# Hybrid encoder block on one core: p's projection moved two experts later, overflow buffer moved

## The chip, the cores and the metric

The kernel runs on one core of one Trainium2 chip. The metric is the device time of one launch in microseconds; the time before is the median of three runs. Everything is float32.

## The reference, cut to what matters

One layer, 512 tokens of 1024 values. After a pooling and state-space mixer, 32 experts follow (4 groups of 8), of which each token takes two; then a gated projection of a side input p, and a last norm:

```python
    h = h + concat([a, s]) @ W_out
    h = h + HierarchicalMoE(RMSNorm(h))      # top-1 group, then top-2 experts in it
    gate = jax.nn.sigmoid(rmsnorm(h, g_ple[i]) @ ple_gate_w[i] + ple_gate_b[i])
    h = h + gate * (p[i] @ ple_proj_w[i])    # p: 512 x 256, ple_proj_w: 256 x 1024
return rmsnorm(h, g_final)
```

An expert is `silu(v @ w_gate) * (v @ w_up) @ w_down` with w_gate and w_up of 1024 x 256 and w_down of 256 x 1024. The change concerns `p[i] @ ple_proj_w[i]`, which depends on nothing else in the layer.

## The kernel before, in words

The five engines each have a program written out by hand; the order of the work on an engine is the order of its code, and semaphores join the engines. The stage that matters is the loop over the 32 experts (`for e in range(1, NE)` at L1980 on TensorE).

Each expert gets a slot of 64 token rows (`CAP`). Its weights come as three pieces of 1 MB (gate, up, down), 96 in all; SyncE issues them in order (`weights`, `load_piece`, L356), each as soon as the buffer that it goes to has been used up (`SPOT`, `AFTER`). The tokens' rows are gathered for two experts at a time by GpSimd (`gather`, L1499) and each expert's result of 128 x 512 values is scattered to DRAM by GpSimd (`scatter`, `rows_out`, L1504) from one of three buffers (`M_Y`, `e % YBUF`). This is done for experts 0 to 29; experts 30 and 31 are combined on TensorE from their buffers (`combined`).

TensorE's steps, all through the helper of L1578 unless another line is given: `gu_step(e)` is the gate and up product (16 matmuls of 64 x 256), `h_step(e)` a transpose (L1940), `down_step(e)` the down product (4 matmuls of 64 x 512), `x_step` 8 transposes of token rows for the next two experts (L1921). One turn of the loop is `h_step(e)`, `x_step` on even e, `gu_step(e + 1)`, now and then a piece of p's work, `down_step(e)`. The trace records every float32 matmul of the products twice (a `gu_step` is x32, a `down_step` x8), a transpose once.

p's work in the loop: at e = 19 (`P_ROWS`) p is transposed (`p_rows`, L1888). At e = 21, 23, 25 and 27 (`P_PROJ`) two half tiles of the projection are computed (`proj`, 2 x 2 matmuls of 128 x 512, banks 0 and 6 of `PP_BANK`, x8 in the trace). ScalarE copies each half tile to zbuf (`pp_out`, L529), between `silu` of the next expert (L752) and the copy of this expert's result (`y_out`, L529). The next `x_step` uses the same banks and waits for these copies (`pp_done`, L1986). The result is read only in the last stage (L1572, L1358).

Behind the experts: GpSimd waits until all scatters have landed and sets `moe_done` by a memset (L1567). SyncE waits for `moe_done` and for `down_step(30)` and then issues the read back of the scattered pairs (`load_pairs(0)`, L492), half of the gate's weights, and the rest. VectorE adds the pairs to h (`combine`, L1330, then L854 with the product of experts 30 and 31), TensorE turns h (`turned_h`, L2036), VectorE scales it to ut (L854), and `gate(0)` to `gate(7)` follow on TensorE.

If an expert has more than 64 tokens, a second loop of rounds follows on every engine (behind `most(...) > CAP`). It gathers, computes and scatters through one slot.

Of the kernel before, what the change touches and what calls it, by code (L numbers as in the profile page):

```python
# [50 lines left out]
NE = NG * NEG  # L51
# [5 lines left out]
PIECE = 2048  # L57
NPIECE = 22
LOADS = 8
YBUF = 3  # L60
# [38 lines left out]
def at(t, parts, off, dims):  # L99

    p0, p1 = parts
    width = t.shape[1]
    return bass.AP(t, p0 * width + off, [[width, p1 - p0]] + [list(d) for d in dims])


def dr(a, off, dims):

    return bass.AP(a.tensor, off, [list(d) for d in dims])
# [25 lines left out]
def build(nc, A, out):  # L134
    ctx = ExitStack()
    with ctx:
        def sb(name, width, dt=F32):
            return ctx.enter_context(nc.sbuf_tensor(name, [P, width], dt))

        def sem(name):  # L140
            return ctx.enter_context(nc.semaphore(name))
# [4 lines left out]
        ALL = (0, P)  # L146
# [6 lines left out]
        moe = sb("moe", 6144)  # L153
# [11 lines left out]
        sidx_o = sb("sidx_o", 1, I32)  # L165
# [5 lines left out]
        bank = [ctx.enter_context(nc.psum_tensor(f"bank{k}", [P, 512], F32)) for k in range(8)]  # L171
# [33 lines left out]
        M_XT, M_SG, M_HT, M_Y, M_XG = 0, 2048, 2304, 2560, 4096  # L205
# [5 lines left out]
        for name, n in (("pr", NT * 32), ("pa", 2 * NT * 32), ("px", NT * 32), ("gm", NT), ("d4", NT * 4), ("e4", NT * 4), ("gs", NT), ("gp", NT),  # L211
# [60 lines left out]
        xT_ps, xT_sb, gu_ps, sg_sb, hg_sb, hT_ps, hT_sb, dn_ps, dn_sb = (  # L272
            sem(n) for n in ("xT_ps", "xT_sb", "gu_ps", "sg_sb", "hg_sb", "hT_ps", "hT_sb", "dn_ps", "dn_sb"))

        o_w, o_tbl, o_idx, o_xg, o_st, o_turn = (sem("o_" + n) for n in ("w", "tbl", "idx", "xg", "st", "turn"))
# [21 lines left out]
                    at(bank[Y_BANK[b]], ALL, 0, [[P, 4], [CH, L], [1, CH]]))  # L297

        PP_BANK = (0, 6)
        P_ROWS, P_PROJ = 19, (21, 23, 25, 27)  # L300
        H_BANK = (0, 2, 4, 2)

        ROOT3 = tuple(NT + t + 1 for t in range(NT))
# [17 lines left out]
        E_PPW, E_PIN, E_PPT = 10 * PIECE, 11 * PIECE, 11 * PIECE + NT * DPLE  # L321
        NA = NT - 1
        E_WPLE = (8 * PIECE, 0)
        O_SLOT = 3 * PIECE
        E_S = E_PIN
        M_GF, M_BP = 4096, 5120

# [21 lines left out]
        def most(eng):  # L349

            return eng.value_load(at(flag, (0, 1), 0, [[1, 1]]), min_val=0, max_val=T)

        def load_piece(eng, e, k, to, done):

            w = (wg_d, wu_d, wd_d)[k]
            eng.dma_start(at(to[0], ALL, to[1], [[1, PIECE]]),  # L356
                          w[e].rearrange("(p j) f -> p (j f)", p=P)).then_inc(done, 16)
# [7 lines left out]
        def _(sp):  # L365
# [106 lines left out]
            with sp.If(most(sp) > CAP):  # L472
                with sp.Fori(1, ROUNDS) as r:
                    with sp.Fori(0, NE) as e0:
# [3 lines left out]
                        for k in range(3):  # L478
                            load_piece(sp, e, k, (ring, O_SLOT + k * PIECE), o_w)
                sp.wait_ge(o_w, 48 * NE * (ROUNDS - 1))  # L480
# [45 lines left out]
        def _(act):  # L526

            def copy(o, i, signal):
                act.activation(o, i, ACT.Copy).then_inc(signal, 1)  # L529
# [260 lines left out]
            with act.If(most(act) > CAP):  # L790
                act.wait_ge(dn_sb, NE)
                with act.Fori(1, ROUNDS) as r:
                    with act.Fori(0, NE) as e:
                        turn = act.snap((r - 1) * NE + e + 1)
                        count = act.snap(turn + NE)
                        act.wait_ge(gu_ps, count)
                        act.activation(at(moe, (0, CAP), M_SG, [[1, DE]]), at(bank[1], (0, CAP), 0, [[1, DE]]),
                                       ACT.Silu).then_inc(sg_sb, 1)
                        act.wait_ge(dn_ps, count)
                        copy(at(moe, ALL, M_Y, [[1, 512]]), bank[4][:, :], dn_sb)  # L800
            with act.Else():
                pass

# [596 lines left out]
        def _(pool):  # L1400
# [97 lines left out]
            def rows_in(k, index, done):  # L1498
                pool.indirect_dma_start(at(moe, ALL, M_XG + k * DM, [[1, DM]]), None, v_d,  # L1499
                                        bass.IndirectOffsetOnAxis(ap=index, axis=0),  # L1500
                                        bounds_check=T - 1, oob_is_err=False).then_inc(done, 16)

            def rows_out(k, index, done):
                pool.indirect_dma_start(pairs, bass.IndirectOffsetOnAxis(ap=index, axis=0),  # L1504
                                        at(moe, ALL, M_Y + k * 512, [[1, 512]]), None,
                                        bounds_check=4 * T - 1, oob_is_err=False).then_inc(done, 16)
# [27 lines left out]
            def note(k):  # L1534

                return pool.tensor_tensor(at(fill, (0, 1), 4 + k, [[1, 1]]), at(fill, (0, 1), 0, [[1, 1]]),
                                          at(fill, (0, 1), 1, [[1, 1]]), ALU.add)

            with pool.If(most(pool) > CAP):
                pool.wait_ge(slot_done, 1)  # L1540
                for c in range(2 * NT):
                    pool.indirect_dma_start(tbl_d, bass.IndirectOffsetOnAxis(ap=slot_i[:, c:c + 1], axis=0),
                                            pair_i[:, c:c + 1], None).then_inc(tbl_set, 16)
                pool.wait_ge(tbl_set, 16 * 2 * NT)
                note(3).then_inc(o_turn, 1)
                with pool.Fori(1, ROUNDS) as r:
                    with pool.Fori(0, NE) as e:
                        turn = pool.snap((r - 1) * NE + e + 1)
                        dma16 = pool.snap(turn * 16)
                        both = pool.snap(turn * 2)  # L1550
                        count = pool.snap(turn + NE)
                        place = pool.snap(r * (CAP * NE))
                        pool.wait_ge(o_turn, turn)
                        for k in range(2):
                            pool.dma_start(at(tblw, (k * CAP, (k + 1) * CAP), 0, [[1, NE]]),
                                           dr(tbl_d, place, [[NE, CAP], [1, NE]])).then_inc(o_tbl, 16)
                        pool.wait_ge(o_idx, both)
                        note(0)
                        rows_in(0, gidx_o[:, 0:1], o_xg)
                        pool.wait_ge(dn_sb, count)  # L1560
                        note(1)
                        rows_out(0, sidx_o[:, 0:1], o_st)
                        pool.wait_ge(o_st, dma16)
                        note(2).then_inc(o_turn, 1)
            with pool.Else():
# [10 lines left out]
        def _(pe):  # L1576
# [349 lines left out]
            def gate_up(k, odd, gate_w, up_w, dst, rows=0, between=None):  # L1926

                for j in range(KC):
                    if rows and j % 4 == 0:
                        pe.wait_ge(xT_sb, rows - 1 + j // 4)  # L1930
                    if between and j == 4:
                        between()
                    for n, w in enumerate((gate_w, up_w)):
                        last = mm(bank[dst][n * CAP:(n + 1) * CAP, 0:DE],
                                  at(moe, ALL, M_XT + k * DM + j * P + odd * CAP, [[1, CAP]]),
                                  at(w[0], ALL, w[1] + j * DE, [[1, DE]]), j == 0, j == KC - 1)
                return last
# [4 lines left out]
            def down(k, w, dst):  # L1942

                for j in range(2):
                    for n in range(2):
                        last = mm(bank[dst][n * CAP:(n + 1) * CAP, :], at(moe, ALL, M_HT + k * P + j * CAP, [[1, CAP]]),
                                  at(w[0], ALL, w[1] + j * DM + n * 512, [[1, 512]]), j == 0, j == 1)
                return last
# [48 lines left out]
            with pe.If(most(pe) > CAP):  # L1997
                with pe.Fori(1, ROUNDS) as r:
                    with pe.Fori(0, NE) as e:
# [9 lines left out]
                        pe.wait_ge(o_w, dma48)  # L2009
                        gate_up(0, 0, (ring, O_SLOT), (ring, O_SLOT + PIECE), 1).then_inc(gu_ps, 1)  # L2010
                        pe.wait_ge(hg_sb, h_count)
                        h_rows().then_inc(hT_ps, 1)
                        pe.wait_ge(hT_sb, count)
                        down(0, (ring, O_SLOT + 2 * PIECE), 4).then_inc(dn_ps, 1)
                pe.wait_ge(dn_sb, NE * ROUNDS)
# [57 lines left out]
```

## Time and profile before

| | us |
|---|---|
| median of 3 runs | 526.2 |
| lowest and highest | 523.4, 529.41 |
| the profiled execution's own time | 522.91 |
| its span, first to last instruction | 521.0 |
| TensorE busy in the span | 480.7 (92%) |
| VectorE, ScalarE, GpSimd busy | 240.9, 163.3, 159.8 |
| moved by DMA | 146.83 MB, mean 282 GB/s |
| mean granted TensorE clock | 0.984 |

The profile is of one execution. Its time is 1.9 us more than its span, and 3.3 us below the median of the three runs, which lie 6 us apart. A duration that is read from it belongs to the 522.91 us; a difference that is worked out from it is laid on the median.

### The profile page before, as it was taken

The page shows a single profiled execution, that of the slowest core. Times are in us where ns is not written, and L with a number is a line of the kernel's source. Part 1 is how long each engine was busy: PE and PEld are TensorE (multiplying, and loading weights), DVE is VectorE, ACT ScalarE, POOL GpSimd, SP SyncE. Part 2 cuts the span into 40 slices and gives each one's busy share as a digit, 9 for nine tenths or more (in the row PEclk, how much of TensorE's full clock was granted, in tenths as well). Part 3 has the DMA queues.
Part 4 walks back from the last instruction along what each step waited for, and adds up shares of the span by engine and source line. Part 5 has one row for each costly group of instructions (what it writes and reads, how often), then busy time and mean ns, then how long its engine had stood idle before and what let it go on. Part 6 is the DMA issues. An engine that isn't in the chain of part 4 may idle for free.

```text
span 521.0 us, 7294 instructions
## 1 busy us (share of the span) xinstructions
PE 480.7 (92%) x2743; PEld 270.9 (52%) x2743; DVE 240.9 (46%) x683; ACT 163.3 (31%) x264; POOL 159.8 (31%) x144
## 2 busy tenths in 40 slices
PE   0999999999999998979999999787999998899993
PEld 0655776734854477745555555444545543444441
DVE  2899998999233358642222222111111211474525
ACT  5643334456442344111111111121121121313464
POOL 1069999954100111222222222202102210003250
PEclk9999999999999999999999999998899998999998
DMA  8784300499289966999999999999999997970012
GB/s 297 141 195 87 75 0 1 147 141 209 110 340 423 414 274 226 403 410 405 422 416 419 419 414 412 422 417 419 423 418 418 419 418 300 350 307 0 0 81 81
DMA packets 57195, 146.83 MB, mean 282 GB/s; under 512 B 27722, under 2 KB 32870, under 8 KB 44360
## 3 DMA queue, kind: packets, MB, share of 16 engines
q1 hardware_dynamic: 50856, 133.92, 69.2%
q0 software_dynamic: 5904, 12.41, 6.2%
q8 instruction: 22, 0.36, 0.3%
q14 instruction: 13, 0.11, 0.1%
q10 hardware_dynamic: 400, 0.04, 0.1%
HBM read 138.17 MB, written 16.29 MB: 296 GB/s over the span
## 4 chain that ended last, share of the span: by engine, by line
PE 75%; DMA 17%; DVE 3%; ACT 2%; SPq 1%; issue 1%; ACTq 0%; DVEq 0%
PE bank L1578 68%; DMA big<-in_exp_w_up_dram 10%; DMA ring<-in_exp_w_up_dram 6%; PE bank L1921 2%; PE bank L1663 1%; DMA ring<-in_ssm_a_im_dram 1%; SPq L356 1%; PE bank L1940 1%; PE bank L1601 1%; ACT moe L529 1%; DVE moe L854 1%; PE bank L1807 1%; PE bank L2036 1%; DVE moe L1091 1%; ACT L537 0%
## 5 line engine op out<-in xcount | busy, mean ns | idle before, releaser
L1578 PE MATMUL bank<-ring,moe 128*64 128x256 f32 (+3 forms) x976 | 130.1, 392 | 3.3 <-DMA ring<-in_exp_w_up_dram 3.3
L1578 PEld LDWEIGHTS bank<-ring,moe 128*64 128x64 f32 (+1 forms) x976 | 76.9, 147 | 39.9 <-issue 17.2
L1504 POOL DMA_INDIRECT pairs_d<-moe,sidx_all x32 | 31.9, 998 | 160.5 <-PE bank L1921 81.6
L854 DVE TENSOR_TENSOR vrow<-moe,bank 64x128 f32<-64x128 f32 x64 | 18.6, 291 | 123.2 <-ACT moe L752 122.2
L1578 PE MATMUL bank<-big,ut 128*128 128x512 f32 x128 | 56.6, 595 | 1.0 <-ACT ut L674 1.0
L1578 PE MATMUL bank<-ut,big 128*128 128x512 f32 x128 | 57.4, 596 | 0.2 <-ACT ut L541 0.2
L752 ACT ACTIVATE moe<-bank 64x256 f32<-64x256 f32 x32 | 12.1, 378 | 143.2 <-PE bank L1578 143.2
L1578 PE MATMUL bank<-ring,ut 128*128 128x512 f32 x128 | 55.7, 593 | 0.4 <-DVE ut L854 0.4
L529 ACT ACTIVATE moe<-bank 128x512 f32<-128x512 f32 x56 | 32.6, 598 | 62.1 <-PE bank L1578 49.4
L1578 PE MATMUL bank<-big,moe 128*64 128x256 f32 (+1 forms) x264 | 44.9, 448 | 6.3 <-DMA zbuf<-in_exp_w_up_dram 3.1
L854 DVE TENSOR_TENSOR ring<-ring,bank 128x64 f32<-128x64 f32 (+1 forms) x142 | 39.5, 278 | 2.8
L1578 PEld LDWEIGHTS bank<-big,ut 128*128 128x128 f32 x128 | 23.9, 190 | 30.9 <-issue 30.6
L1578 PEld LDWEIGHTS bank<-ring,ut 128*128 128x128 f32 x128 | 24.0, 190 | 29.3 <-issue 29.3
L1578 PEld LDWEIGHTS bank<-ut,big 128*128 128x128 f32 x128 | 23.4, 190 | 25.5 <-issue 24.7
L854 DVE TENSOR_TENSOR bank<-bank,ring 128x64 f32<-128x64 f32 (+1 forms) x142 | 35.1, 287 | 2.9
L1578 PEld LDWEIGHTS bank<-big,moe 128*64 128x64 f32 x264 | 22.5, 145 | 22.0 <-issue 7.7
L1578 PE MATMUL bank<-ring 128*64 128x128 f32 (+1 forms) x128 | 32.5, 437 | 0.0
L1267 DVE COPY moe<-bank 128x128 f32<-128x128 f32 x32 | 9.3, 292 | 45.5 <-PE bank L1940 45.5
L854 DVE TENSOR_TENSOR moe<-bank,vec 128x512 f32<-128x512 f32 x40 | 25.9, 686 | 7.2 <-PE bank L1921 5.2
L1578 PEld LDWEIGHTS bank<-ring 128*64 128x64 f32 (+1 forms) x128 | 15.2, 163 | 15.3 <-issue 15.0
L1572 POOL TENSOR_TENSOR ring<-ring,zbuf 128x512 f32<-128x512 f32 x6 | 8.1, 1349 | 48.1 <-ACT ring L815 48.1
L529 ACT ACTIVATE zbuf<-bank 128x512 f32<-128x512 f32 x16 | 11.5, 718 | 34.5 <-PE bank L1578 34.5
(190 smaller groups left out, 605.5 us busy)
## 6 DMA issues: line engine op xcount, KB each, us to landing
ring<-in_exp_w_up_dram SPq DMA_DIRECT2D x19, 1024.0 KB, 30.2
ring<-in_exp_w_down_dram SPq DMA_DIRECT2D x18, 1024.0 KB, 29.9
ring<-in_exp_w_gate_dram SPq DMA_DIRECT2D x17, 1024.0 KB, 26.2
big<-in_exp_w_gate_dram SPq DMA_DIRECT2D x7, 1024.0 KB, 13.4
big<-in_exp_w_down_dram SPq DMA_DIRECT2D x7, 1024.0 KB, 12.8
big<-in_exp_w_up_dram SPq DMA_DIRECT2D x6, 1024.0 KB, 16.0
big<-in_w_in_dram SPq DMA_DIRECT2D x2, 2048.0 KB, 11.8
ut<-in_exp_w_gate_dram SPq DMA_DIRECT2D x4, 1024.0 KB
```

What stands on the lines that cost most here:

```text
L356: eng.dma_start(at(to[0], ALL, to[1], [[1, PIECE]]), w[e].rearrange("(p j) f -> p (j f)", p=P)).then_inc(done, 16)
L529: act.activation(o, i, ACT.Copy).then_inc(signal, 1)
L752: act.activation(at(moe, (0, CAP), M_SG, [[1, DE]]), at(bank[1 + e % 2], (0, CAP), 0, [[1, DE]]), ACT.Silu).then_inc(sg_sb, 1)
L854: return dve.tensor_tensor(o, a, b, op)
L1091: return dve.scalar_tensor_tensor(o, a, b, c, op0, op1)
L1267: dve.tensor_copy(at(moe, ALL, M_HT + (e % 2) * P, [[1, P]]), bank[3][:, 0:P]).then_inc(hT_sb, 1)
L1504: pool.indirect_dma_start(pairs, bass.IndirectOffsetOnAxis(ap=index, axis=0), at(moe, ALL, M_Y + k * 512, [[1, 512]]), None, bounds_check= ...
L1572: seq(pool.tensor_tensor(sg, sg, at(zbuf, ALL, n * 512, [[1, 512]]), ALU.mult))
L1578: return pe.matmul(o, a, b, start=start, stop=stop, skip_group_check=loose)
L1601: last = pe.transpose(bank[j][:, t * P:(t + 1) * P], at(moe, ALL, M_XN + t * DM + j * P, [[1, P]]), ident)
L1663: last = pe.transpose(bank[B_WT + ri][:, (g % 4) * P:(g % 4 + 1) * P], rv(R_W + ri * 1024 + g * P, P), ident)
L1921: last = pe.transpose(bank[j // 4 * 6][:, (j % 4) * P:(j % 4 + 1) * P], at(moe, ALL, M_XG + k * DM + j * P, [[1, P]]), ident)
```

## The change

Two things. The four pairs of half tiles of p's projection are computed at e = 23, 25, 27 and 29 in place of 21, 23, 25 and 27, on TensorE and, with their copies, on ScalarE. In the loop for overfull experts, the result goes through buffer 2 of `M_Y` (29 % 3) in place of buffer 0, on ScalarE and GpSimd.

```diff
         PP_BANK = (0, 6)
-        P_ROWS, P_PROJ = 19, (21, 23, 25, 27)
+        P_ROWS, P_PROJ = 19, (23, 25, 27, 29)
...
-        O_SLOT = 3 * PIECE
+        O_SLOT, O_Y = 3 * PIECE, (NE - 3) % YBUF
...
-                        copy(at(moe, ALL, M_Y, [[1, 512]]), bank[4][:, :], dn_sb)
+                        copy(at(moe, ALL, M_Y + O_Y * 512, [[1, 512]]), bank[4][:, :], dn_sb)
...
-                        rows_out(0, sidx_o[:, 0:1], o_st)
+                        rows_out(O_Y, sidx_o[:, 0:1], o_st)
```

On TensorE, in the turn of e = 21: 64x256 x16 is `gu_step(22)`, 128x512 x4 the two half tiles, 64x512 x4 `down_step(21)`, L1940 `h_step`.

```order
 L1940 MATMUL bank<-cst,vrow 128x128
 L1578 MATMUL bank<-ring,moe 64x256 x16
-L1578 MATMUL bank<-ring 128x512 x4
 L1578 MATMUL bank<-ring,moe 64x512 x4
 L1940 MATMUL bank<-cst,vrow 128x128
```

The half tiles are gone from here. The rows of e = 23, 25 and 27 read the same in both kernels, though they hold other half tiles.

On TensorE, in the turn of e = 29, of the kernel after the change: `h_step(29)`, `gu_step(30)`, half tiles, `down_step(29)`, `h_step(30)`, then `gu_step(31)` and `down_step(30)`.

```order
 L1940 MATMUL bank<-cst,vrow 128x128
 L1578 MATMUL bank<-ring,moe 64x256 x16
+L1578 MATMUL bank<-ring 128x512 x4
 L1578 MATMUL bank<-ring,moe 64x512 x4
 L1940 MATMUL bank<-cst,vrow 128x128
```

The last two half tiles now stand between `gu_step(30)` and `down_step(29)`, and so ahead of `gu_step(31)`.

On ScalarE, the end of the loop in the kernel after the change: `silu(30)`, the two `pp_out`, `y_out(29)`, `silu(31)`, `y_out(30)` and `y_out(31)`.

```order
L752 ACTIVATE moe<-bank 64x256
L529 ACTIVATE zbuf<-bank 128x512 x2
L529 ACTIVATE moe<-bank 128x512
L752 ACTIVATE moe<-bank 64x256
L529 ACTIVATE moe<-bank 128x512 x2
```

In the kernel before, nothing stands there between `silu(30)` and `y_out(29)`. The programs of VectorE, GpSimd and SyncE keep their order.

## Rows read from the trace of the kernel before

**Rows 1.** Page, 40 slices of the span: granted clock and DMA share in tenths.
```profile
PEclk9999999999999999999999999998899998999998
DMA  8784300499289966999999999999999997970012
```
**Rows 2.** Waits of TensorE, 300 to 521 us: us in total, times, longest.
```profile
PE bank L1578 <- DMA ring<-in_exp_w_up_dram: 3.3, 2, 3.1
PE bank L1578 <- DMA big<-in_exp_w_up_dram: 2.9, 2, 2.6
```
**Rows 3.** Timeline of TensorE: start, duration, line, tiles, records [idle before].
```profile
361.74 6.46 PE L1578 MATMUL bank<-ring,moe 128*64 128x256 f32 x32 [3.06 <-DMA ring<-in_exp_w_up_dram]
368.13 3.70 PE L1578 MATMUL bank<-ring 128*128 128x512 f32 x8
...
411.97 3.67 PE L1578 MATMUL bank<-ring,moe 128*64 128x256 f32 x32
415.58 3.70 PE L1578 MATMUL bank<-ring 128*128 128x512 f32 x8
419.21 1.94 PE L1578 MATMUL bank<-ring,moe 128*64 128x512 f32 x8
421.08 0.33 PE L1940 MATMUL bank<-cst,vrow 128*128 128x128 f32 x1
...
428.05 5.39 PE L1578 MATMUL bank<-ring,moe 128*64 128x256 f32 x40 [0.19 <-DMA ring<-in_exp_w_up_dram]
...
436.30 6.75 PE L1578 MATMUL bank<-big,moe 128*64 128x256 f32 x40 [2.59 <-DMA big<-in_exp_w_up_dram]
```
**Rows 4.** Stretches, TensorE: length, busy, granted clock, DMA share, GB/s.
```profile
343.30:346.00 2.70, 0.73 (x8) 1.00 1.01 416
346.00:352.00 6.00, 6.00 (x46) 1.00 1.01 417
...
434.00:436.30 2.30, 0.00 (x1) 0.87 1.01 404
436.30:439.00 2.70, 2.70 (x14) 0.50 0.77 305
439.00:441.80 2.80, 2.80 (x26) 0.98 0.45 176
```
**Rows 5.** The chain that ended last, up to the gate: start, us, what.
```profile
405.17 31.09 DMA big<-in_exp_w_up_dram
...
446.42 7.21 PE bank L1578 x32
453.63 0.60 PE bank L2036 x4
```
**Rows 6.** Timeline of VectorE behind the experts.
```profile
449.18 2.99 DVE L1330 SCALAR_TENSOR_TENSOR h<-big,small,h 128x512 f32<-128x512 f32 x4 [5.54 <-DMA big<-pairs_d]
452.28 1.29 DVE L854 TENSOR_TENSOR h<-bank,h 128x512 f32<-128x512 f32 x2
454.25 1.29 DVE L854 TENSOR_TENSOR ut<-bank,vec 128x512 f32<-128x512 f32 x2 [0.69 <-PE bank L2036]
...
462.67 1.29 DVE L854 TENSOR_TENSOR ut<-bank,vec 128x512 f32<-128x512 f32 x2 [2.64 <-PE bank L2036]
```
**Rows 7.** Instructions on the scattered pairs: ns min/median/max, first and last start.
```profile
L1504 POOL DMA_INDIRECT pairs_d<-moe,sidx_all x32: 982/992/1043, 226.7 to 434.9; - x32
```
**Rows 8.** Timelines of ScalarE and GpSimd at the last scatter.
```profile
433.49 0.60 ACT L529 ACTIVATE moe<-bank 128x512 f32<-128x512 f32 x1 [1.34 <-PE bank L1578]
...
434.86 0.98 POOL L1504 DMA_INDIRECT pairs_d<-moe,sidx_all  x1 [4.86 <-ACT moe L529]
441.79 0.09 POOL L1567 MEMSET fill<- 1x1 int32 x1 [5.95 <-issue]
```
**Rows 9.** Timeline of SyncE: the issue of the first pairs.
```profile
443.14 0.34 SPq L492 DMA_DIRECT2D big<-pairs_d  x1
```
**Rows 10.** DMA issues, 300 to 521 us: count, KB each, us to landing.
```profile
out_dram<-ring SPq DMA_DIRECT2D x2, 256.0 KB, 2.0
```

## The prediction

> **What bounds the kernel now.** I read the page first. Its slices show DMA busy at 9 tenths from about the middle to slice 33 and TensorE's clock full but for a few slices [rows 1]: the expert stage sits close to both limits. Next come TensorE's waits in the second part of the span: it waits only for expert weights, a few us in all [rows 2]. Then the timeline places them [rows 3]: 3.06 us ahead of gu_step(22) at 361.74, 0.19 ahead of gu_step(30) at 428.05, and 2.59 ahead of gu_step(31) at 436.30. Between 361.74 and 428 TensorE never waits, so there it is the bound by a hair; at either end the weights are. From gu_step(22) to gu_step(31) are 9 experts in 436.30 - 361.74 = 74.56 us, 8.28 us each. As both of these starts are landings of weights, 8.28 us is the pace at which an expert's 3 MB arrive; it puts gu_step(30)'s at 361.74 + 8 x 8.28 = 428.0, where the row has 428.05. The DMA share of 1.01 in a sample stretch [rows 4] agrees. The piece that gu_step(31) waits for was issued at 405.17 and took 31.09 us to land [rows 5]: a long queue, so what TensorE does a few us earlier or later does not change when weights land.
>
> The chain that ended last then goes straight through TensorE: the combination of experts 30 and 31 from 446.42, turning h from 453.63, then VectorE's scaling at 454.25 and the gate's products [rows 5, 6]. About that place VectorE matters too: the pairs land and it starts at 449.18, and it is done with h at 452.28 + 1.29 = 453.57 [rows 6], within 0.1 us of when TensorE is free at 453.63. Two chains arrive there together, and the change lengthens one of them.
>
> **The change, part by part.** Overflow buffer: costs nothing. There are 32 scatters in the trace [rows 7], which are the 30 of experts 0 to 29 and the two of zeros ahead of them, so the loop for overfull experts does not run; one constant changes in it.
>
> Half tiles out of e = 21: 415.58 to 419.21 is 3.63 us for two half tiles in front of down_step [rows 3]. The same work at 368.13 to 371.8 goes. TensorE then has 3.63 us in hand from there on. It can't keep them: at the arrival pace of 8.28 us per expert, gu_step(24)'s weights land at 378.3, those for 26 at 394.9, for 28 at 411.4. gu_step(28) starts at 411.97 [rows 3], only 0.5 us behind that. So the lead is given back as small waits in front of gu_step(24), (26), (28) and (30). For gu_step(30) I work this out: from gu_step(28) to being ready for gu_step(30) takes 428.05 - 0.19 - 411.97 = 15.89 us; from 411.45 that is 427.3, a wait of 0.7 us for 428.05. If nothing had been given back the wait would be 0.19 + 3.63 = 3.8 us. I take 0.7, since the pace holds within 0.1 us at gu_step(30). The SyncE issues behind these steps gain nothing, by the queue of 31 us.
>
> Half tiles into e = 29: gu_step(30) starts at 428.05 as before, since it waits for weights. It takes 3.61 us (411.97 to 415.58), then half tiles 3.63, down_step(29) 1.87 (419.21 to 421.08), and some 0.26 for h_step(30) (0.33 by its row at 421.08, of which the next step covers a little). That is 428.05 + 9.37 = 437.42 for gu_step(31). Its weights have been there since 436.30. Cover of 2.59 us plus what is left of it: the half tiles are hidden but for 1.12 us.
>
> The clock: before, gu_step(31) and down_step(30) took 6.75 us for the 40 records that take 5.39 warm [rows 3], because the granted clock is 0.50 in that stretch, which is 1.2 GHz, right behind the idle 2.59 us [rows 4]. After, TensorE works from 428.05 to 443 without a gap over 0.1 us, so I price this at 5.33 us plus nothing: 1.36 us won back. down_step(30) ends at 437.42 + 5.33 = 442.75, where before it was 436.30 + 6.75 = 443.05. The new wait of 0.7 us ahead of gu_step(30) I price at nothing: an idle 1.98 us up to 345.27 left the clock at 1.00, in the stretch of the gap and in the one behind it [rows 4]. On TensorE alone the change comes to -0.3 us.
>
> The last scatter: this is what pays. ScalarE's copy of expert 29's result starts when down_step(29) ends, at 433.49 before, and the scatter at 434.86 [rows 8], 1.37 us later. Now down_step(29) ends at 437.16, the copy starts at 437.27 (both pp_out are over by 436.1, 0.6 us each, behind half tiles that end by 435.3), and the scatter at 438.64, 3.78 us later. Before, GpSimd's memset followed the scatter's start by 6.93 us (0.98 of work and 5.95 idle until it landed) [rows 8], and at 441.79 it was 1.2 us earlier than needed, since SyncE also waits for down_step(30) and issued the pairs at 443.14 [rows 9]. Now: with the same 6.93 us the memset is at 445.57 and the pairs are issued at 445.7, 2.6 us late. From the other side, a store of 256 KB, as large as the scatter, landed in 2.0 us when DMA had nothing else to move [rows 10]; then the memset is at 441.6, down_step(30) decides again, and the issue is 0.3 us early. The DMA load behind 438.6 lies between: share 0.77 up to 439.0, 0.45 up to 441.8, against 1.01 around the old scatter's start [rows 4]. The nearest row is the old scatter itself, with the same rows, queue and target, so I stay by its side and take 5.0 us to landing: memset at 444.6, pairs issued at 444.8, 1.65 us late. The rule of the Trainium skill (DMA: Bandwidth & Descriptors, "Anatomy of one DMA") gives a DMA some 2.0 us and its bytes at 436 GB/s, 2.6 us here, by which the scatter would land ahead of down_step(30) and the whole change would be worth -0.3 us; the 5.95 us of the trace speak against it, with load on the engines.
>
> What follows: the pairs land 1.65 us later, VectorE starts at 450.8 and has h done at 455.2 in place of 453.57. It scaled h at 454.25 before, held by TensorE's transposes for 0.68 us [rows 5, 6]; this slack is used up first. gate(0) therefore starts 1.65 - 0.68 = 1.0 us later. Behind it TensorE is the bound, as the loads issued behind the pairs move by the same 1.65 us, and VectorE stood idle for 2.64 us ahead of the next tile's scaling [rows 6].
>
> The sum: TensorE -0.3, hidden behind the pairs' +1.0; so 522.91 + 1.0 = 523.9 for an execution like the profiled one, and 526.2 + 1.0 = 527.2 on the median. The median lies 3.3 us above the profiled execution, and its runs 6 us apart. What a measurement of this kernel can tell from no change is about 1%, 5.3 us, five times my figure. Bounds of the terms: pairs from -0.3 to +2.6 - 0.7 = +1.9 us.
>
> **The rivals.**
> *The half tiles are fully covered (A).* If the scatter lands in 3 us or less, or if the last weights are late by some us more (the median execution is 3.3 us longer than the profiled one, and DMA is the natural cause), down_step(30) decides the issue of the pairs and TensorE's own balance counts: -0.3 us to -1.4 us with the clock kept, 525.5 us. For it: DMA load falls off just there. Against it: 5.95 us of landing.
> *The clock and the pairs (B, slower).* The place is gate(0). If TensorE's wait ahead of gu_step(30) is long enough to bring the clock down there (it is up to 3.8 us if weights come unevenly; 3.06 us ahead of gu_step(22) did, with 6.46 us for what takes 3.67 [rows 3]), gu_step(31) is 1.36 us later still. The scatter too, so that with its old 6.93 us the pairs are issued 2.6 + 1.4 = 4.0 us late and gate(0) starts 3.3 us late. TensorE has by then been idle for over 2.6 us, and pays 1.4 to 2.8 us of low clock in gate(0), the prices of the falls at 436.30 and 361.74. Sum +4.7 to +6.1, 531.6 us. It decides where the wait ahead of gu_step(30) has grown from my 0.7 us to one like that of 2.59 us, which the low clock followed, and is no longer like that of 1.98 us. The Trainium skill (TensorE: Matmul & The Clock Gate, Part 1) says that where the clock turns varies from run to run of the same kernel; by that some executions pay and some don't. No run yet shows this.
> *The weights come earlier (C).* If TensorE's lead of 3.63 us freed buffers that SyncE waits for, the last weights could land up to 3.6 us earlier: -2.5 us, 523.7 us. Against it: 31 us from issue to landing of the last one [rows 5]; a queue that long is not short of issues.
>
> **How the numbers follow.** Forecast 0.50 (527.2, own range 525.9 to 528.1), A 0.28, B 0.12, C 0.05, something unforeseen 0.05. The range must hold the medians' own scatter, whose three runs span 523.4 to 529.41, laid about A to B: 523.2 to 531.0. Slower by over 1% (above 531.5): half of B and a little noise, 0.08. Faster by over 1% (below 520.9): hardly reached even by C, 0.04 with noise. The rest, 0.88, is within 1%.
>
> **What would show it.** Right, step by step, if in the profile of the changed kernel the wait of about 3 us ahead of gu_step(22) stands, gu_step(24), (26), (28) and (30) have waits of 0.5 to 1.6 us, gu_step(31) has none and takes 3.6 us at clock 1.00; if the last scatter starts 3.8 us later, the memset follows it by about 6 us, and the pairs are issued by it and not by down_step(30); and if VectorE's wait for the pairs ends 1 to 2 us later. Wrong if gu_step(31) still waits (then weights come later than I hold), if the memset is ahead of down_step(30)'s end (A), if the clock is 0.50 in gu_step(30) or in gate(0) (B), or if the last weights land more than 1 us earlier (C).

## The result, and the profile after

| | before | after |
|---|---|---|
| median of 22 executions each, us | 523.58 | 527.38 |
| lowest and highest | 522.78, 529.41 | 523.74, 532.52 |
| profiled execution, us | 522.91 | 527.45 |
| its span | 521.0 | 525.5 |

The ratio after to before is 1.0049, with a 95% interval from 1.0028 to 1.0069: 1.5 to 3.6 us slower, some 2.6 us. The ratio leaves the two slowest executions after the change (531.73 and 532.52) out; the bare medians lie 3.8 us apart. That is inside 1% and on the side that was forecast, but the forecast step was +1.0 us. The forecast 527.2 us lies near the measured 527.38 only because the three runs it started from had a high median; over 22 executions the kernel before has 523.58.

The timeline of TensorE after the change, the rows that answer to [rows 3]:

```profile
365.21 8.15 PE L1578 MATMUL bank<-ring,moe 128*64 128x256 f32 x40 [3.08 <-DMA ring<-in_exp_w_up_dram]
...
381.42 3.67 PE L1578 MATMUL bank<-ring,moe 128*64 128x256 f32 x32 [1.35 <-DMA ring<-in_exp_w_up_dram]
...
397.71 3.67 PE L1578 MATMUL bank<-h,moe 128*64 128x256 f32 x32 [0.41 <-DMA h<-in_exp_w_up_dram]
...
414.91 3.67 PE L1578 MATMUL bank<-ring,moe 128*64 128x256 f32 x32 [1.32 <-DMA ring<-in_exp_w_up_dram]
...
431.71 3.67 PE L1578 MATMUL bank<-ring,moe 128*64 128x256 f32 x32 [0.91 <-DMA ring<-in_exp_w_up_dram]
435.31 3.70 PE L1578 MATMUL bank<-ring 128*128 128x512 f32 x8
438.94 1.94 PE L1578 MATMUL bank<-ring,moe 128*64 128x512 f32 x8
441.07 5.39 PE L1578 MATMUL bank<-big,moe 128*64 128x256 f32 x40
...
458.11 1.26 PE L2036 MATMUL bank<-cst,h 128*128 128x128 f32 x8 [1.07 <-DVE h L854]
459.64 7.11 PE L1578 MATMUL bank<-ring,ut 128*128 128x512 f32 x16 [0.27 <-DVE ut L854]
```

This execution reaches gu_step(22) at 365.21 in place of 361.74, 3.47 us later, in a part of the program that the change does not touch; so I measure from gu_step(22) on. The half tiles are gone from e = 21 (the row runs on as x40). The lead is given back in four waits of 1.35, 0.41, 1.32 and 0.91 us, ahead of gu_step(24), (26), (28) and (30). gu_step(31) starts 441.07 - 431.71 = 9.36 us behind gu_step(30), with no wait, and takes 5.39 us, no longer 6.75. gate(0) starts 459.64 - 365.21 = 94.43 us behind gu_step(22), where it was 455.09 - 361.74 = 93.35: +1.08 us. In the profiled execution the path behind gu_step(22) is longer by just what was forecast, though two of its terms missed in opposite directions: measured from gu_step(30), the pairs were issued 448.95 - 431.71 = 17.24 us behind it where 16.75 was forecast, and landed in 5.3 us where the profile before, and with it the forecast, has 6.0 (443.14 to 449.18).

The chain that ended last, in the same place, answers to [rows 5]:

```profile
431.71 9.20 PE bank L1578 x48
440.90 0.02 issue
440.93 0.61 ACT moe L529
...
442.30 5.42 DMA pairs_d<-moe,sidx_all
...
447.83 0.50 POOLq L351
...
448.84 0.10 POOL fill L1567
448.94 0.02 issue
448.95 5.29 DMA big<-pairs_d
454.24 0.03 issue
454.27 0.76 DVE h L1330
...
458.11 0.67 PE bank L2036 x4
```

Before, the chain stayed on TensorE through gu_step(31) and the combination. Now it leaves TensorE behind down_step(29), which is late by the half tiles, and goes through ScalarE's copy, the last scatter, GpSimd's memset, the load of the pairs and VectorE, and comes back to TensorE at turned_h(0). TensorE's own steps beside it have time to spare: it waits 1.07 us there.

### The profile page after: what moved, and what is told of

It reads as the page before. It is cut to its first block, busy times and chain, and to the rows that moved or that the text cites. A ratio compares the mean times of both kernels' runs of the same rounds, so it can differ in the third digit from the quotient of the medians.

```text
span 525.5 us, 7294 instructions
## 1 busy us (share of the span) xinstructions
PE 482.3 (92%) x2743; PEld 271.9 (52%) x2743; DVE 240.8 (46%) x683; ACT 163.3 (31%) x264; POOL 160.6 (31%) x144
## 4 chain that ended last, share of the span: by engine, by line
PE 69%; DMA 23%; DVE 4%; ACT 2%; issue 1%; ACTq 0%; POOLq 0%; DVEq 0%; SPq 0%; POOL 0%
PE bank L1578 63%; DMA ring<-in_exp_w_up_dram 11%; DMA h<-in_exp_w_up_dram 6%; DMA moe<-v_d,gidx_all 2%; DMA ring<-in_ssm_a_im_dram 1%; PE bank L1921 1%; PE bank L1663 1%; PE bank L1601 1%; DMA pairs_d<-moe,sidx_all 1%; DMA big<-pairs_d 1%; PE bank L1940 1%; DVE moe L854 1%; PE bank L1807 1%; PE bank L2036 1%; DVE h L1330 1%
## 5 line engine op out<-in xcount | busy, mean ns | idle before, releaser
L1578 PE MATMUL bank<-big,moe 128*64 128x256 f32 (+1 forms) x264 | 43.5, 435 | 3.6 <-DMA zbuf<-in_exp_w_up_dram 3.2
L1578 PE MATMUL bank<-zbuf,moe 128*64 128x256 f32 (+2 forms) x80 | 22.3, 494 | 0.0
```

The source lines that it names most:

```text
L1578: return pe.matmul(o, a, b, start=start, stop=stop, skip_group_check=loose)
```

## The experiments

Three theories stood against each other. S: the loss is the last scatter, late because the last half tiles stand ahead of down_step(29). K: it is the new small waits on TensorE, behind which the clock falls. N: S, and whatever is over +1.0 us is chance in the front part. After the first four runs S was widened to SV: the late scatter also lays bare delays in landing that were hidden before.

**e1, only the overflow buffer moved.**

```diff
-        P_ROWS, P_PROJ = 19, (23, 25, 27, 29)
+        P_ROWS, P_PROJ = 19, (21, 23, 25, 27)
```
(against the kernel after)

> Only the overflow buffer moves; p's projection stays at 21, 23, 25, 27. All theories: same time as before within 0.2% (1 us). It serves as the measure of how two equal kernels differ in their medians. If it is 2 us or more slower, the buffer's number is not free after all, or the way the instructions lie in memory is.

Measured: 523.5 us median, ratio 1.0003 (0.9978 to 1.0029). The buffer's number costs nothing that can be seen, and this is how well two kernels with the same steps agree: to -1.2 to +1.5 us.

**e2, only the last pair of half tiles moved.** Again against the kernel after:

```diff
-        P_ROWS, P_PROJ = 19, (23, 25, 27, 29)
+        P_ROWS, P_PROJ = 19, (21, 23, 25, 29)
```

> Pairs at 21, 23, 25 and 29: only the last pair of half tiles moves, from 27 to 29. Theory S (down_step(29) and with it the last scatter are late): the scatter starts 3.8 us later than the end of gu_step(30) plus 3.2 us, and gate(0) is 1.0 to 1.9 us late, as after the change: +1.0 us and more. Theory K (small waits ahead of gu_step(24), (26), (28) and (30) bring the clock down in many executions): waits ahead of (24), (26) and (28) are gone here, one of up to 3 us stands ahead of gu_step(29) or (30) instead, so at most one fall of the clock, +1 to +2.5 us. Theory N (the rest of the difference is chance in the front part): +1.0 us.

Measured: 527.6 us, ratio 1.0068 (1.0038 to 1.0098). One pair moved from 27 to 29 gives the whole loss and perhaps more. The small waits ahead of gu_step(24), (26) and (28) are absent here, so they are not needed for the loss. That does not yet rule K out as the cause, since e2 has waits of its own ahead of gu_step(29) and (30); e3 and e4 do that. And +3.6 us is more than S gave. The timeline of TensorE in e2's profile, which is of the slowest of its ten executions (531.75 us):

```profile
430.99 5.36 PE L1578 MATMUL bank<-ring,moe 128*64 128x256 f32 x32 [2.32 <-DMA ring<-in_exp_w_up_dram]
...
460.70 1.25 PE L2036 MATMUL bank<-cst,h 128*128 128x128 f32 x8 [2.69 <-DVE h L854]
```

gu_step(30) takes 5.36 us in place of 3.67 behind a wait of 2.32 us, and the wait for the pairs is 2.69 us in place of 1.07. The way from gu_step(22) to the second tile's transposes is 6.1 us longer than before here, by these two steps and the low clock behind each.

**e3, the last pair behind down_step(29).** Against the kernel after; ScalarE's copies are moved in the same way.

```diff
+                if e == 29:
+                    down_step(e)
                 if e in P_PROJ:
                     for n in range(2):
                         proj(e, 2 * P_PROJ.index(e) + n)
-                down_step(e)
+                if e != 29:
+                    down_step(e)
```

> Pairs at 23, 25, 27, 29 as after the change, but the last pair stands behind down_step(29) on TensorE, and its copies behind the result's copy on ScalarE. The half tiles are still in front of gu_step(31). Theory S: the scatter starts as early as before, moe_done precedes down_step(30)'s end, gate(0) is 0.3 us earlier than before: -0.3 us to 0. Theory K: the small waits stand as after the change, so it stays 2 to 3 us slower than before. Theory N: as S.

Measured: 524.16 us, ratio 1.0006 (0.9979 to 1.0033). TensorE has the same work between the same landings of weights as after the change, with waits of 0.98, 0.61 and 1.34 us ahead of gu_step(24), (26) and (28) in its profile, and the loss is gone. The scatter is early again, 6.81 us behind gu_step(30) as before. The timeline of TensorE in e3's profile:

```profile
364.05 8.29 PE L1581 MATMUL bank<-ring,moe 128*64 128x256 f32 x40 [3.06 <-DMA ring<-in_exp_w_up_dram]
...
439.65 5.39 PE L1581 MATMUL bank<-big,moe 128*64 128x256 f32 x40
...
457.08 7.10 PE L1581 MATMUL bank<-ring,ut 128*128 128x512 f32 x16 [0.44 <-DVE ut L857]
```

gate(0) is 457.08 - 364.05 = 93.03 us behind gu_step(22), 0.32 us less than before, close to the forecast -0.3 us for TensorE alone. The agreement is in part chance: in e3's order gu_step(31) follows gu_step(30) by 9.06 us and not by 9.36, and the way from gu_step(22) to gu_step(30) took 0.23 us more than before. Either is too small to be seen in the medians.

**e4, the kernel before with the last scatter put off.** On GpSimd, ahead of scatter(29), a dead buffer is cleared:

```diff
+                if e == 29:
+                    pool.wait_ge(xT_ps, 2 * (NE // 2))
+                    pool.wait_ge(dn_sb, e + 1)
+                    for _ in range(4):
+                        seq(pool.memset(at(moe, ALL, M_XG, [[1, DM]]), 0.0))
                 scatter(e)
```

> The kernel before with one thing added: GpSimd clears a dead buffer four times ahead of the last scatter, which puts the scatter off by about 4 us; nothing moves on TensorE. Theory S: the pairs are issued about 2.5 to 3 us later than before, gate(0) starts 1.5 to 2.3 us later (the scatter is put off from a step that is not late itself), and the time is +1.5 to +2.5 us. Theory K and any other that puts the loss on TensorE's own steps: no more than +0.5 us.

Measured: 528.11 us, ratio 1.0077 (1.0049 to 1.0104), with nothing moved on TensorE. The timelines of GpSimd and of TensorE in e4's profile:

```profile
441.04 0.99 POOL L1504 DMA_INDIRECT pairs_d<-moe,sidx_all  x1 [0.78 <-POOL moe L1534]
```
```profile
438.37 6.80 PE L1583 MATMUL bank<-big,moe 128*64 128x256 f32 x40 [2.59 <-DMA big<-in_exp_w_up_dram]
```

The scatter starts at 441.04, 2.67 us behind the start of gu_step(31) at 438.37; before it was 1.44 us ahead, so it is 4.11 us late. The late scatter alone makes at least the whole loss: 4.0 us, 2.6 to 5.4 by the interval, above the expected +1.5 to +2.5. The profile does not show all of it: it is of an execution of 525.87 us, in which the pairs landed in 5.0 us and gate(0) came 0.9 us later than before, counted from gu_step(31).

**e6, the same with two clears.** `range(2)` for `range(4)`.

> As e4, with two clears in place of four: the last scatter is about 2.6 us late in place of 4.8 us (two clears of 1 us and 0.8 us of waiting fewer than four take). Theory SV with a threshold: before, the memset stood 1.2 us ahead of need and VectorE had 0.7 us of slack, so 1.9 us are free; the pairs come some 1.3 us late and gate(0) 0.7 us, and a late sixteenth part of the pairs costs up to 1.5 us more: median +0.5 to +2 us, under half of what e4 lost. A theory in which any lateness counts in full gives half of e4's +4.2 us or more.

Measured: 523.61 us, ratio 0.9994 (0.9969 to 1.0019). From e6's profile, the timeline of GpSimd and, behind it, that of VectorE:

```profile
438.68 0.99 POOL L1504 DMA_INDIRECT pairs_d<-moe,sidx_all  x1 [0.78 <-POOL moe L1534]
445.47 0.09 POOL L1572 MEMSET fill<- 1x1 int32 x1 [5.80 <-issue]
```
```profile
456.05 1.29 DVE L854 TENSOR_TENSOR ut<-bank,vec 128x512 f32<-128x512 f32 x2 [0.99 <-PE bank L2041]
```

The scatter is 438.68 - 437.91 = 0.77 us behind gu_step(31)'s start in place of 1.44 ahead, 2.2 us late, and it costs nothing. In this execution the pairs took 5.1 us to land, and VectorE waited 0.99 us for TensorE; with the 6.0 us of the profile before, this slack would have been just used up. So 2.2 us of lateness are free within the interval (-1.6 to +1.0 us, below the expected +0.5 to +2), 3.8 us cost 2.6 us (1.5 to 3.6) and 4.1 us cost 4.0 us (2.6 to 5.4): a threshold. How steeply the cost rises behind it, these overlapping intervals do not tell.

**c1, c2 and c3, the kernel after the change again.** Three more profiles of single executions, on a chip on which the kernel before has a median of 525.01 us; so their distances are compared and not their times.

> The kernel after the change once more, for its profile. Theory S alone: gate(0) starts 94.3 to 94.6 us after gu_step(22), in every execution, and an execution that is longer by 2 us or more has lost this ahead of gu_step(22). Theory SV (what lands late now costs in full): that distance varies by 1 to 4 us from one execution to another, with TensorE's wait for the pairs, and where this wait is over 2 us the granted clock is 0.50 for a while in gate(0).

> As c1: a further profile of the kernel after the change. S: gate(0) 94.3 to 94.6 us after gu_step(22). SV: a distance that varies by 1 to 4 us, with the wait for the pairs.

> As c1: a further profile of the kernel after the change. S: gate(0) 94.3 to 94.6 us after gu_step(22). SV: a distance that varies by 1 to 4 us, with the wait for the pairs.

Measured: 528.45, 523.21 and 527.53 us. The rows below show, in c2 and then in c1, the load of the pairs, turned_h(0), gate(0) and turned_h(1). c2 first (its pairs landed 4.9 us after their issue at 445.11):

```profile
453.88 1.25 PE L2036 MATMUL bank<-cst,h 128*128 128x128 f32 x8 [0.64 <-DVE h L854]
455.41 7.11 PE L1578 MATMUL bank<-ring,ut 128*128 128x512 f32 x16 [0.28 <-DVE ut L854]
462.36 1.04 PE L2036 MATMUL bank<-cst,h 128*128 128x128 f32 x8
```

And c1, with the stretches of TensorE around the wait (length, busy, granted clock, DMA share, GB/s):

```profile
445.69 7.17 DMA big<-pairs_d
```
```profile
456.73 1.97 PE L2036 MATMUL bank<-cst,h 128*128 128x128 f32 x8 [2.91 <-DVE h L854]
458.71 9.04 PE L1578 MATMUL bank<-ring,ut 128*128 128x512 f32 x16
467.60 1.04 PE L2036 MATMUL bank<-cst,h 128*128 128x128 f32 x8
```
```profile
456.70:458.70 2.00, 1.97 (x8) 0.50 1.04 387
458.70:462.00 3.30, 3.29 (x4) 0.50 1.07 416
462.00:468.00 6.00, 6.00 (x17) 0.95 0.98 401
```

And the timeline of TensorE in c3:

```profile
457.15 1.97 PE L2036 MATMUL bank<-cst,h 128*128 128x128 f32 x8 [3.18 <-DVE h L854]
459.14 7.70 PE L1578 MATMUL bank<-ring,ut 128*128 128x512 f32 x16
466.68 1.04 PE L2036 MATMUL bank<-cst,h 128*128 128x128 f32 x8
```

The steps up to the issue of the pairs are alike: the scatter starts 10.59 us behind gu_step(30) in all four profiles, and the memset 6.5 us behind the scatter. Then they part. In c1 and c3 the same 1 MB of pairs takes 7.2 and 7.4 us to land, in c2 and in the first profile 4.9 and 5.3. TensorE waits 2.91 and 3.18 us in place of 0.64 and 1.07; and behind the long waits the granted clock is 0.50, which is 1.2 GHz, so gate(0) takes 9.04 and 7.70 us in place of 7.11. The price, taken to the start of turned_h(1) and against the 462.04 - 361.74 = 100.30 us before:

| profile | pairs landed in, us | wait for pairs | gu_step(22) to turned_h(1) | against before |
|---|---|---|---|---|
| c2 | 4.9 | 0.64 | 101.05 | +0.75 |
| after | 5.3 | 1.07 | 101.37 | +1.07 |
| c3 | 7.4 | 3.18 | 104.61 | +4.31 |
| c1 | 7.2 | 2.91 | 105.78 | +5.48 |

What holds of SV: two of these four pay about the forecast +1 and two pay 4 to 5, and the difference is the landing of the pairs with the clock behind it. The middle of the four, (1.07 + 4.31) / 2 = 2.7 us, is near the measured 2.6, but four profiles are few and this may be chance. In the 22 executions, 5 lie at 523.7 to 524.5, one step of 1 us above the kernel before at its best, and the other 17 from 526.5 up, where the kernel before has 4 of 22. These 17 are not all late pairs: gu_step(22) itself starts between 361.31 and 365.21 us in the four profiles, so the front part moves by as much.

What is not shown is the "hidden before". In the six profiles in which the pairs are issued early, 13.8 to 15.8 us behind the start of gu_step(30) (before, e1, e3, e5, e6, e7), they landed in 5.1 to 6.3 us. All five landings of 6.8 us or more are among the eight in which they are issued late, 17.2 to 18.9 us behind it (after, c1, c2, c3, c4, e2, e4, e8). So the long landing may have come with the late issue.

**e8 and c4, the pairs loaded alone.** What delays the pairs? SyncE issues the gate's second half 0.4 us behind them. Here it waits until the pairs have landed:

```diff
             load_pairs(0)
+            sp.wait_ge(ld_pairs[0], 16)
             load_gate(0, 4, 4, ld_wple)
```

> The kernel after the change, but SyncE waits until the first tile of pairs has landed before it issues the gate's second half and the rest. Theory Q (the loads issued right behind the pairs crowd one of the sixteen engines, and so the pairs land after 7.2 to 7.4 us in some executions and 5 us in others): they always land in about 5 us, TensorE's wait ahead of turned_h(0) stays near 1 us, and the median is that of the good executions of the kernel after, +1 us against before, if the gate's weights, now issued 5 us later, still land ahead of gate(0)'s second half. Theory I (something apart from these loads holds one engine up): the pairs still take over 7 us in part of the executions and the median stays 2.5 to 4 us above before.

> e8 once more, for a second profile. Q: pairs land in 4.9 to 5.4 us. I: the one or the other, as chance has it.

Measured: e8 526.26 us, ratio 1.0032 (0.9997 to 1.0066), c4 526.15 us. Rows of the chain in e8's profile and, behind them, in c4's:

```profile
448.74 6.98 DMA big<-pairs_d
```
```profile
446.12 6.83 DMA big<-pairs_d
```

The pairs take about 7 us with nothing issued behind them, so theory Q, that the loads issued behind the pairs delay them, falls. In the landings that the trace records for each sixteenth of the transfer, 15 are there within 0.5 us, and the last is over 2 us later, in c1, c3, e2, e8 and c4 alike. Why one part is late, and why only in some executions, is not settled.

One candidate was not tested. In this stretch each trace has one packet of 16 KB on the queue that the profile calls "q8 instruction". In the eight profiles with a late issue it starts 0.1 to 0.7 us behind the issue of the pairs, ahead of their transfer or beside its first packets; in the six others 4.4 to 6.2 us behind it, towards the end of the transfer. But it stands in the same place in after, c2 and e4, whose pairs landed in 4.9 to 5.3 us, so alone it does not explain the late part.

c4 also shows a wait of 2.58 us for the pairs with the clock at 1.00 behind it, and gate(0) at 7.11 us:

```profile
456.81 1.26 PE L2037 MATMUL bank<-cst,h 128*128 128x128 f32 x8 [2.58 <-DVE h L855]
458.34 7.11 PE L1579 MATMUL bank<-ring,ut 128*128 128x512 f32 x16 [0.28 <-DVE ut L855]
```

**e5 and e7, two tries at a faster kernel.** e5 is e3, and the first two tiles of pairs go to two pieces of `ring` that are free since expert 29, so that their load waits for moe_done alone. The cut shows SyncE's part; VectorE reads the two tiles from their new place:

```diff
             sp.wait_ge(moe_done, 1)
-            sp.wait_ge(dn_ps, NE - 1)
             load_pairs(0)
             load_gate(0, 4, 4, ld_wple)
-            sp.wait_ge(gu_ps, NE)
             load_pairs(1)
+            sp.wait_ge(dn_ps, NE - 1)
+            sp.wait_ge(gu_ps, NE)
```

> The order of e3 (last half tiles behind down_step(29)), and the first two tiles of pairs are read back into ring pieces 6 and 7, free since expert 29, so that their load waits for moe_done alone and no longer for down_step(30) and gu_step(31). Theory S (pairs and TensorE meet at turned_h(0) with no margin): a margin of over 1 us arises on the side of the pairs, TensorE never waits for them, and executions in which the scatter or the pairs land late cost nothing. Median 0 to -1 us against before, and fewer executions above 525. If the spread of the kernel before comes from its front part, the spread stays.

Measured: 523.74 us, ratio 0.9978 (0.9955 to 1.0001), with a highest execution of 526.3 where the kernel before, on the same chip, had 527.47. The timelines of VectorE and of TensorE in e5's profile:

```profile
450.09 2.99 DVE L1337 SCALAR_TENSOR_TENSOR h<-ring,small,h 128x512 f32<-128x512 f32 x4 [4.82 <-DMA ring<-pairs_d]
```
```profile
455.20 1.09 PE L2046 MATMUL bank<-cst,h 128*128 128x128 f32 x8
```

VectorE starts on the pairs at 450.09 while TensorE is free at 455.20, a margin of 0.7 us behind VectorE's 4.4 us of work. The interval just includes no change, so a gain is not shown.

e7 is e5 with the last pair split: half tiles 0 to 5 at 21, 23 and 25, half tile 6 at 27, and 7 at 29 behind down_step(29).

> Half tiles at 21, 23, 25 in pairs, one at 27 and one at 29, the last behind down_step(29), with the pairs read back early as in e5. Of the 2.59 us ahead of gu_step(31) one half tile fills 1.8 us, so gu_step(31) starts when its weights land, as before, but at full clock: 1.36 us gained on TensorE, and the pairs are issued at moe_done, 1.2 us earlier than before, so VectorE is ready too. Theory SV: -1.2 us against before, -1 to -2 us in the median, and few executions above 525. If the clock falls anyway, or another load is the next to be late, no more than -0.3 us.

Measured: 524.59 us, ratio 1.0002 (0.9976 to 1.0029): nothing gained where -1 to -2 us were expected. The timeline of TensorE in e7's profile:

```profile
428.54 7.08 PE L1584 MATMUL bank<-ring,moe 128*64 128x256 f32 x40 [2.33 <-DMA ring<-in_exp_w_up_dram]
437.57 5.39 PE L1584 MATMUL bank<-big,moe 128*64 128x256 f32 x40
```

With half the work gone from e = 27, TensorE reaches gu_step(30) 2.33 us ahead of its weights, the clock falls there (7.08 us for 5.39, 1.69 us more), and so more was lost one step earlier than the 1.36 us won at gu_step(31). The idle time was moved, not filled.

## Why the prediction was right, and where it was off

*What bounds the kernel.* Right. The pace of the weights held: 8.31 us per expert from gu_step(22) to (30) after the change, (431.71 - 365.21) / 8, against the 8.28 read. The weights of gu_step(30) did not come earlier, so rival C fell.

*Overflow buffer at nothing.* Right as far as can be seen, e1: 1.0003.

*Half tiles out of e = 21: the lead given back in small waits.* Right in the profiled execution and in c2: four waits, 0.91 us ahead of gu_step(30) for a forecast 0.7. In c1 and c3, which are the same kernel, the longest wait stood ahead of gu_step(24) and was 3.40 and 2.96 us; in c4, e5 and e8, which share this part of the program, it was 3.37, 3.24 and 2.71 us. In c4 and e5 gu_step(24) then took 6.30 and 6.59 us for 3.67, and gu_step(30) started 67.23 and 67.59 us behind gu_step(22) in place of 66.31, with no wait: there the clock behind a wait, K's mechanism, cost TensorE 0.9 and 1.3 us, for which the prediction has no term. In c3 and e8 a fall of the clock at gu_step(24) cost nothing by gu_step(30). Over all executions e3 bounds it: the same waits, and a median within -1.1 to +1.7 us of before.

*Half tiles into e = 29: 9.37 us from gu_step(30) to gu_step(31), hidden but for 1.12 us.* Right: 9.36 us. The clock's 1.36 us came back as forecast (5.39 for 6.75). TensorE alone, counted from gu_step(30): down_step(30) ended 0.25 us earlier (14.75 us for 15.00), for the forecast 0.3; at turned_h(0) TensorE was ready 0.18 us earlier (458.11 - 1.07 - 431.71 = 25.33 us behind gu_step(30), for 25.51).

*The last scatter.* Right in start, 10.59 us behind gu_step(30) for a forecast 438.64 - 428.05 = 10.59, and right that moving it is what pays: e2 and e4 lose without the rest, e3 has the rest and does not lose. Its way to the memset was mis-sized, and this error met that of the pairs' landing. I took the idle time of 5.95 us before for landing; 1.1 us of the way from the scatter's start to the memset, behind the landing, is GpSimd's own reading and branching (from 447.72, when the scatter of the profile has landed, to 448.84). From start to memset I had 6.0 us, and it took 6.5 in each of the four profiles. The rule of the Trainium skill (DMA: Bandwidth & Descriptors, "Anatomy of one DMA"), 2.0 us and the bytes at 436 GB/s, gives an estimate of 2.6 us here. This trace does not agree: it has 5.4, and the measurement decides.

*What follows from it: this is the step that failed.* The prediction had "the pairs land 1.65 us later", with the time from issue to landing kept at that of the one profile, and gate(0) "therefore 1.0 us later" at full clock. That landing time is no constant: it was 6.0 us in the profile before, and 4.9 to 7.4 us in the eight profiles whose pairs were issued late. It is luck that the profiled execution came out at +1.08: pairs that landed 0.7 us sooner than forecast made up for the 0.5 us by which they were issued later than forecast. Where they landed late, every bit of it reached TensorE, and the low clock followed behind the wait in four of five such profiles (c1, c3, e2 and e8, not c4). The term was sized +1.0 us and measured 2.6 (1.5 to 3.6), a median over executions of which some pay about 1 and some 4 to 5. Why a landing is long stays open.

*The rivals.* A did not happen: in none of the four profiles of this kernel was the memset ahead of down_step(30)'s end. B named the right place and its second half, TensorE idle at gate(0) and the clock at 0.50 behind it; but its beginning was wrong. I let it hang on a fall of the clock at gu_step(30), and in c1 and c3 it came about without one, through the pairs alone. That is why I gave 0.12 to what happened in two of the four profiles of this kernel. The whole of B, with its beginning, stands in one profile, e2's: 2.32 us of wait and the low clock at gu_step(30), 2.69 us of wait and the low clock at gate(0), and 6.1 us in sum, the upper end of B's +4.7 to +6.1.

## What to carry to other kernels

When work is moved into a wait, list what is queued behind it on the engine that is filled: here 3.6 us of matmuls covered a wait of 2.6 us at a cost of 1.1, but a small step behind them fed a scatter, and a store of 5.4 us and a load of 5 to 7 us hung on that. Put the filler behind the step that starts a long chain, not ahead of it; e3 is the same change without its cost. Where two chains meet with less margin than the spread of a DMA's landing, a median can move by more than the one profile shows, so profile several executions before you size a term.

## What was not expected of the hardware

The load of 1 MB from DRAM took 4.9 to 7.4 us to land from one execution of the same kernel to the next, by one late part of sixteen. How long TensorE idled did not alone decide whether the clock fell: the low clock followed waits of 2.32 (e2), 2.33 (e7), 2.69 (e2), 2.82 (e8), 2.91 and 3.18 us (c1, c3), but not one of 2.58 us (c4), and not one of 3.40 us in c1, behind which gu_step(24) took its full-clock 3.67 us:

```profile
379.00 3.67 PE L1578 MATMUL bank<-ring,moe 128*64 128x256 f32 x32 [3.40 <-DMA ring<-in_exp_w_up_dram]
```

The Trainium skill (TensorE: Matmul & The Clock Gate, Part 1) says of the rise to full clock that its point shifts from run to run of one kernel. These rows show the like for the fall.
